# Experts' sums taken slot by slot, 64 columns of TensorE at a time, instead of two slots side by side

## The chip, the cores and the metric

One core of a Trainium2 chip runs the whole program. The metric is the device time of one execution in microseconds (us), with the median of several runs. Engines are TensorE (PE, with its weight loads PEld), VectorE (DVE), ScalarE (ACT), GpSimd (POOL) and SyncE (SP). They run their own instruction lists in order and are tied together by semaphores alone. DMA queues carry the transfers.

## What is computed

Two layers of a backbone over 256 latent tokens and 256 context tokens, 1024 channels. Each layer has a mixer (an input projection, a pooling mixer, latent attention, a bidirectional mLSTM, an output projection) and then an expert layer. The expert layer is what the first edit touches:

```python
def peer_ffn(h, w_q, subkeys, u_tab, v_tab):          # per block of 128 tokens
    q = (hb @ w_q).reshape(P, 8, 2, 128)
    s = einsum('phcd,hcnd->phcn', q, subkeys)         # 128 keys, two halves, 8 heads
    ...                                               # top 16 of 16 x 16 pairs -> 16 experts a head
    expert = i1 * 128 + i2
    a = gelu(einsum('pd,phkd->phk', hb, u_tab[expert]))
    w = softmax(best) * a
    return einsum('phk,phkd->pd', w, v_tab[expert])   # 8 x 16 = 128 experts a token
```

The second edit touches one RMS norm over the 384 channels of the low-rank query, `rms_norm(zq, q_a_norm)`, a mean of squares over three blocks of 128 channels.

## The kernel before

**Slots.** Tokens are held in tiles of 128. A tile has 128 slots: in each, 128 rows of 8 KB (u and v side by side, 1 MB in all) are gathered by an indirect DMA into one buffer (L546, `gather`). A slot serves 64 tokens with two heads' experts, so two neighbouring slots (an even and an odd one) serve the two halves of the tile. For every slot `dot` (L1269, VectorE) multiplies the u half with the tokens' rows and sums; `gated` (L844, L845, L848, ScalarE) makes the gate, the coefficient and `diag`, a 128x64 matrix that carries the coefficients; `values` (L1668, TensorE) multiplies `diag` with the v half and adds into `acc`, the even slot into its partitions 0 to 63 and the odd one into 64 to 127. A 1024-column row takes two matmuls of 512 columns; a float32 matmul is two records in the profile, each with a weight load. After the 128 slots of a tile ScalarE copies `acc` out (`sums_out`) and starts the next tile.

**Two loops.** `experts(0)` (layer 0) has four tiles, 512 slots, and a ring of six buffers (`fast`). `experts(1)` (layer 1) has two tiles, 256 slots, and twelve buffers (`fast` and six cut from `mix`). `v_used` counts slots whose sums are done; `free_pair(m)` is the count that frees slot m's buffer. It is awaited by the gather that reuses a buffer (L545), by ScalarE before it writes one of the eight `diag` again (L847), and by six weight loads of SyncE behind the last slots (L511).

**Work behind the slots.** In the first loop the rest of the program runs behind the slots: the mixer of the latent tokens of layer 0, the adaLN product of layer 1 (24 weight tiles), and the context's keys and values of layer 1. Each engine has these parts written as generators that yield the slot after which a step may be issued, and `behind.run(m)` issues all that is due. Positions: projections at slots 12 to 59 (three steps to a group of eight matmuls, L1404), memory stage of four heads 63 to 92, row products 98 to 122, attention 127 to 165, output projection 167 to 190, adaLN 206 to 253, a shorter mixer's norm and projections 272 to 313. The expert layer's query products (L1627) lie between slots too, a whole product at a time split in pieces, 0 to 47, 203 to 303, in the second loop 0 to 47. From slot 314 on there is nothing but the slots. TensorE's order in a slot is: key scores, query piece, tile turns, `behind.run(m)`, then at an odd m `values(e, m - 1)` for both slots of the pair.

**The norm.** `low_rank` on ScalarE squares the three blocks of `zqT` (two buffers `sq`: the third square waits until TensorE has used the first), on TensorE `sum_square` (L1376) adds them, on VectorE `mean` and `inverse` turn the sum into a factor, with ScalarE's `root` between. `at` is slot 42 for this norm in the mixer behind the slots.

Of the kernel before, what the change touches and what calls it, by code (L numbers as in the profile page):

```python
# [15 lines left out]
D = 1024  # L16
# [24 lines left out]
SLOTS = PH * PTOP  # L41
HALF = P // 2
# [15 lines left out]
DIAGS = 8  # L58
# [15 lines left out]
def groups(p):  # L74
    return GROUPS if PHASES[p][2] else KV_GROUPS


def group_of(p, name, n):
    return [g[:2] for g in groups(p)].index((name, n)) + 1
# [23 lines left out]
def in_at(g):  # L103
    return IN_AT + IN_STEP * g
# [160 lines left out]
def build(nc, x_in, c_in, par_in, con_in, w_in, wq_in, uq_in, pw_in, uv_tabs, out):  # L265
    with ExitStack() as ctx:
        def sb(name, shape, dt=F32):
            return ctx.enter_context(nc.sbuf_tensor(name, shape, dt))
# [4 lines left out]
        def signal(name, *counts):  # L273
            return Signal(ctx, nc, name, counts)

        bank = [ctx.enter_context(nc.psum_tensor(f"bank{i}", [P, 512], F32)) for i in range(6)]
        acc = ctx.enter_context(nc.psum_tensor("bank67", [P, 1024], F32))
# [27 lines left out]
        diag = sb("diag", [P, DIAGS, HALF])  # L305
# [71 lines left out]
        def slot(e, m):  # L377
            return rings[e][m % len(rings[e])]
# [15 lines left out]
            return 4 if PHASES[p][1] == 0 else 2  # L394

        def free_pair(m):
            return 2 * (m // 2) + 2


        c_loaded, con_loaded, loaded = sem("c_loaded"), sem("con_loaded"), sem("loaded")  # L400
# [51 lines left out]
        def each(n):  # L452
            return [n * nt for nt in nts]
# [5 lines left out]
        dotted, diag_ready, v_used = (signal(n, *each(SLOTS)) for n in ("dotted", "diag_ready", "v_used"))  # L459
# [96 lines left out]
        def _(a):  # L556
# [7 lines left out]
            def square(p, n, src):  # L564
                if n >= 2:
                    a.wait_ge(sq_used.sem, sq_used.at(p, n - 1))
                a.activation(sq[:, n % 2, :], src, ACT.Square).then_inc(sq_ready.sem, 1)

            def root(p, n):
                a.wait_ge(ms_ready.sem, ms_ready.at(p, n))  # L570
                a.activation(rms[:, :], rms[:, :], ACT.Sqrt).then_inc(rt_ready.sem, 1)
# [90 lines left out]
            def low_rank(p):  # L662
                at = in_at(group_of(p, "zkv", 1) - 1) + 3
                yield at + 1
                a.wait_ge(in_evac.sem, in_evac.at(p, group_of(p, "zkv", 1)))
                for k in range(2):
                    square(p, KC + k, zkvT[:, k, :])
                yield at + 5
                root(p, 2)
                if PHASES[p][2]:  # L670
                    at = in_at(group_of(p, "zq", 2) - 1) + 3
                    yield at + 1
                    a.wait_ge(in_evac.sem, in_evac.at(p, group_of(p, "zq", 2)))
                    for k in range(3):
                        square(p, KC + 2 + k, zqT[:, k, :])
                    yield at + 5
                    root(p, 3)

            def pooled(p):
# [230 lines left out]
        def _(v):  # L910
# [36 lines left out]
            def mean(p, n, squares_used, width):  # L947
                v.wait_ge(sq_used.sem, sq_used.at(p, squares_used))
                if n == 1 and p:
                    v.wait_ge(hx_ready.sem, hx_ready.starts[p])  # L950
                if n == 2:
                    v.wait_ge(hx_ready.sem, hx_ready.at(p, KC))
                if n == 3:
                    v.wait_ge(zn_ready.sem, zn_ready.at(p, 2))
                if n == 4:
                    v.wait_ge(zn_ready.sem, zn_ready.at(p, 5))
                v.tensor_scalar(rms[:, :], bank[3][:, 0:SEQ], 1.0 / width, EPS, ALU.mult, ALU.add).then_inc(ms_ready.sem, 1)

            def inverse(p, n):
                v.wait_ge(rt_ready.sem, rt_ready.at(p, n))  # L960
                link(v.reciprocal(rms[:, :], rms[:, :]))
# [48 lines left out]
            def low_rank(p):  # L1010
                l, s, whole = PHASES[p]

                def scaled(z, n, gains):
                    for k in range(n):
                        v.scalar_tensor_tensor(out=z[:, k, :], in0=z[:, k, :], scalar=par[:, l, gains + k:gains + k + 1],
                                               in1=rms[:, :], op0=ALU.mult, op1=ALU.mult).then_inc(zn_ready.sem, 1)

                at = in_at(group_of(p, "zkv", 1) - 1) + 3
                yield at + 4
                mean(p, 2, KC + 2, KVRANK)  # L1020
                yield at + 6
                inverse(p, 2)
                scaled(zkvT, 2, PB_KVN)
                if whole:
                    at = in_at(group_of(p, "zq", 2) - 1) + 3
                    yield at + 4
                    mean(p, 3, KC + 5, QRANK)
                    yield at + 6
                    inverse(p, 3)
                    scaled(zqT, 3, PB_QN)  # L1030

# [283 lines left out]
        def _(t_):  # L1315
# [58 lines left out]
            def sum_square(p, n, first, last):  # L1374
                t_.wait_ge(sq_ready.sem, sq_ready.at(p, n + 1))
                t_.matmul(bank[3][:, 0:SEQ], ones, sq[:, n % 2, :], start=first, stop=last).then_inc(sq_used.sem, 1)  # L1376
# [50 lines left out]
            def low_rank(p):  # L1427
                yield in_at(group_of(p, "zkv", 1) - 1) + 6
                t_.wait_ge(ms_ready.sem, ms_ready.at(p, 1))
                for k in range(2):  # L1430
                    sum_square(p, KC + k, k == 0, k == 1)
                if PHASES[p][2]:
                    yield in_at(group_of(p, "zq", 2) - 1) + 6
                    t_.wait_ge(ms_ready.sem, ms_ready.at(p, 2))
                    for k in range(3):
                        sum_square(p, KC + 2 + k, k == 0, k == 2)

            def pooling(p):
# [214 lines left out]
            def sums_turn(e, i, f):  # L1653
                t_.wait_ge(y_ready.sem, y_ready.at(e, i + 1))
                take_aside(x_part, x_part.at(e, 2 * i + f + 1))
                for j in range(4):
                    mm = t_.transpose(b_aside[:, j * P:(j + 1) * P], yrow[:, (4 * f + j) * P:(4 * f + j + 1) * P], ident)
                mm.then_inc(yt_mm.sem, 1)

            def values(e, m):  # L1660

                if m % SLOTS == 0 and m:
                    t_.wait_ge(y_ready.sem, y_ready.at(e, m // SLOTS))
                t_.wait_ge(diag_ready.sem, diag_ready.at(e, m + 2))
                for f in range(2):
                    for half in range(2):
                        n = m + half
                        mm = t_.matmul(acc[half * HALF:(half + 1) * HALF, f * 512:(f + 1) * 512], diag[:, n % DIAGS, :],  # L1668
                                       slot(e, n)[:, D + f * 512:D + (f + 1) * 512],
                                       start=(n % SLOTS < 2), stop=(n % SLOTS >= SLOTS - 2))  # L1670
                mm.then_inc(v_used.sem, 2)

            def experts(e, behind):
                nt = nts[e]
                answer = {slot_: u for u, slot_ in ASKED[e].items()}
                part_of = {slot_: (u, k0, k1) for slot_, u, k0, k1 in QUERIES[e]}
                query(e, 0, 0, KC)
                query(e, 1, 0, KC)
                for u in range(8):
                    key_scores(e, u)  # L1680
                    if u == 3:
                        for half in range(2):
                            for f in range(2):
                                rows_turn(e, 0, half, f)
                    if u + 2 < 8:
                        query(e, u + 2, 0, KC)
                for m in range(SLOTS * nt):
                    i, n = divmod(m, SLOTS)
                    if m - 2 in answer:
                        key_scores(e, answer[m - 2])  # L1690
                    if m in part_of:
                        query(e, *part_of[m])
                    if i and n == 0:
                        rows_turn(e, i, 1, 1)
                    if i and n in (4, 8):
                        sums_turn(e, i - 1, (n - 4) // 4)
                    if i + 1 < nt:
                        if n == 114:
                            rows_turn(e, i + 1, 0, 0)
                        if n == 117:  # L1700
                            rows_turn(e, i + 1, 0, 1)
                        if n == 124:
                            rows_turn(e, i + 1, 1, 0)
                    behind.run(m)
                    if m % 2:
                        values(e, m - 1)
                for f in range(2):
                    sums_turn(e, nt - 1, f)

# [108 lines left out]
```

## Time and profile before

| | us |
|---|---|
| median of 3 runs | 2892.78 |
| lowest, highest | 2888.32, 2907.57 |
| profiled execution | 2890.09 |
| its span, first to last instruction | 2888.3 |

All rows below come from the one profiled execution, whose time is 1.8 us above its span. Times in them are us from the start of the span. A row of the busy table has for each engine its busy time and the number of records; then PEclk, the clock granted to TensorE as a share of 2.4 GHz (it has two levels, 1.2 and 2.4, so 0.75 is half of the time at either), the mean busy share of the DMA engines, and the rate. Busy is the time in which at least one record of the engine ran, so matmuls that overlap count once. The first loop's dots run from 323 to 1884 and the second's from 2218 to 2872.

### The profile page before, as it was taken

The page shows a single profiled execution, that of the slowest core. Times are in us where ns is not written, and L with a number is a line of the kernel's source. Part 1 is how long each engine was busy: PE and PEld are TensorE (multiplying, and loading weights), DVE is VectorE, ACT ScalarE, POOL GpSimd, SP SyncE. Part 2 cuts the span into 40 slices and gives each one's busy share as a digit, 9 for nine tenths or more (in the row PEclk, how much of TensorE's full clock was granted, in tenths as well). Part 3 has the DMA queues.
Part 4 walks back from the last instruction along what each step waited for, and adds up shares of the span by engine and source line. Part 5 has one row for each costly group of instructions (what it writes and reads, how often), then busy time and mean ns, then how long its engine had stood idle before and what let it go on. Part 6 is the DMA issues. An engine that isn't in the chain of part 4 may idle for free.

```text
span 2888.3 us, 26625 instructions
## 1 busy us (share of the span) xinstructions
PE 2007.8 (70%) x8372; PEld 981.8 (34%) x8372; DVE 1638.7 (57%) x4029; ACT 1123.0 (39%) x3259; POOL 868.1 (30%) x772
## 2 busy tenths in 40 slices
PE   7988598767777777786555555587796865565555
PEld 4756455332343343342111111155574421111111
DVE  2252477668875644676666665432532777776664
ACT  3242263556663433354333333332331443343332
POOL 0000133334354322334344434300001444444442
PEclk9879899878899898898777777786698997787777
DMA  7520499989999999999999999931004999999997
GB/s 311 222 117 17 150 393 412 378 311 372 386 382 411 403 420 421 386 403 394 384 387 369 387 392 391 379 127 46 15 1 154 412 426 426 426 426 426 426 426 303
DMA packets 133660, 940.05 MB, mean 325 GB/s; under 512 B 14864, under 2 KB 16144, under 8 KB 23312
## 3 DMA queue, kind: packets, MB, share of 16 engines
q0 software_dynamic: 110592, 805.36, 69.1%
q1 hardware_dynamic: 22496, 130.31, 11.4%
q10 hardware_dynamic: 432, 2.70, 0.2%
q8 instruction: 66, 1.08, 0.1%
q14 instruction: 74, 0.61, 0.1%
HBM read 937.26 MB, written 1.05 MB: 325 GB/s over the span
## 4 chain that ended last, share of the span: by engine, by line
DMA 42%; PE 32%; DVE 9%; ACT 8%; issue 4%; POOL 4%; POOLq 0%; SPq 0%; DVEq 0%; ACTq 0%
DMA fast<-uv_dram,idx 38%; PE bank L1668 11%; DVE fast L1269 4%; PE bank L1627 4%; PE bank L1404 4%; DMA qring<-wq_dram 3%; POOL fast L546 3%; PE bank L1590 2%; PE bank L1482 2%; ACT diag L848 1%; PE bank L1398 1%; ACT coef L845 1%; PE bank L1637 1%; PE bank L1574 1%; PE bank L1376 1%
## 5 line engine op out<-in xcount | busy, mean ns | idle before, releaser
L546 POOL DMA_INDIRECT fast<-uv_dram,idx x642 | 726.2, 1131 | 1819.4 <-PE bank L1668 1051.9
L1668 PE MATMUL bank<-fast,diag 128*64 128x512 f32 x2568 | 826.7, 777 | 585.7 <-ACT diag L848 585.4
L1269 DVE SCALAR_TENSOR_TENSOR fast<-fast,hrow 128x1024 f32<-128x1024 f32 x642 | 785.8, 1224 | 597.5 <-DMA fast<-uv_dram,idx 590.2
L844 ACT ACTIVATE gact<-araw 128x1 f32<-128x1 f32 x768 | 155.0, 202 | 1089.7 <-DVE fast L1269 922.7
L1668 PEld LDWEIGHTS bank<-fast,diag 128*64 128x64 f32 x2568 | 188.3, 164 | 1110.3 <-ACT diag L848 834.0
L1627 PE MATMUL bank<-hT,qring 128*128 128x256 f32 x768 | 238.7, 443 | 76.6 <-DMA qring<-wq_dram 67.3
L848 ACT ACTIVATE diag<-con,coef 128x64 f32<-128x64 f32 x768 | 267.0, 348 | 25.1
L1668 PE MATMUL bank<-mix,diag 128*64 128x512 f32 x504 | 171.8, 818 | 113.3 <-ACT diag L848 113.3
L845 ACT ACTIVATE coef<-gact,wts 128x1 f32<-128x1 f32 x768 | 226.2, 295 | 24.9
L1627 PEld LDWEIGHTS bank<-hT,qring 128*128 128x128 f32 x768 | 152.2, 215 | 188.0 <-issue 93.6
L1269 DVE SCALAR_TENSOR_TENSOR mix<-mix,hrow 128x1024 f32<-128x1024 f32 x126 | 154.5, 1226 | 98.1 <-DMA mix<-uv_dram,idx 95.2
L546 POOL DMA_INDIRECT mix<-uv_dram,idx x126 | 141.7, 1125 | 161.7 <-PE bank L1668 137.2
L1668 PEld LDWEIGHTS bank<-mix,diag 128*64 128x64 f32 x504 | 38.2, 168 | 235.8 <-ACT diag L848 178.1
L1404 PE MATMUL bank<-hT,back 128*128 128x256 f32 (+1 forms) x336 | 84.0, 389 | 4.1 <-ACT hT L594 4.1
L1404 PE MATMUL bank<-hT,fast 128*128 128x256 f32 (+1 forms) x320 | 76.1, 394 | 4.8 <-ACT hT L594 4.8
L1065 DVE TENSOR_TENSOR mix<-con,bank 128x256 f32<-128x256 f32 x48 | 17.0, 415 | 103.7 <-PE bank L1482 64.0
L1482 PE MATMUL bank<-mix 128*128 128x65 f32 x272 | 54.2, 376 | 30.6 <-DVE mix L1075 30.6
L814 ACT ACTIVATE pq<-bank 128x256 f32<-128x256 f32 x48 | 18.2, 379 | 142.2 <-PE bank L1627 142.1
L1404 PEld LDWEIGHTS bank<-hT,back 128*128 128x128 f32 (+1 forms) x336 | 63.3, 190 | 17.9 <-issue 7.4
L844 ACT ACT_TABLE_LOAD x52 | 66.7, 1283 | 0.9
L1404 PEld LDWEIGHTS bank<-hT,fast 128*128 128x128 f32 (+1 forms) x320 | 61.1, 194 | 16.6 <-issue 7.3
L1482 PEld LDWEIGHTS bank<-mix 128*128 128x128 f32 x272 | 50.9, 286 | 42.3 <-issue 42.3
(222 smaller groups left out, 2337.4 us busy)
## 6 DMA issues: line engine op xcount, KB each, us to landing
fast<-w_dram SPq DMA_DIRECT2D x48, 1024.0 KB, 7.2
back<-w_dram SPq DMA_DIRECT2D x44, 1024.0 KB, 9.9
qring<-wq_dram SPq DMA_DIRECT2D x48, 576.0 KB, 8.2
fast<-uv_dram,idx POOLq DMA_INDIRECT x642, 9.9
fast<-uq_dram SPq DMA_DIRECT2D x4, 576.0 KB, 4.4
xT<-x_dram ACTq DMA_DIRECT2D x1, 2048.0 KB, 8.7
mix<-uv_dram,idx POOLq DMA_INDIRECT x126, 22.2
back<-uq_dram SPq DMA_DIRECT2D x2, 576.0 KB, 8.2
```

The lines of the kernel that those rows point to most:

```text
L546: g.indirect_dma_start(slot(e, m), None, uv_tabs[e], bass.IndirectOffsetOnAxis(idx[:, Q % 2, n:n + 1], 0)).then_inc(landed[m % R], 16)
L844: link(a.activation(gact[:, n:n + 1], araw[:, Q % 2, n:n + 1], ACT.Gelu))
L845: link(a.activation(coef[:, n:n + 1], gact[:, n:n + 1], ACT.Copy, scale=wts[:, Q % 2, n:n + 1]))
L848: a.activation(diag[:, m % DIAGS, :], two, ACT.Copy, scale=coef[:, n:n + 1]).then_inc(diag_ready.sem, 1)
L1269: v.scalar_tensor_tensor(out=u, in0=u, scalar=1.0, in1=hrow[:, (2 * i + half) % 3, :], op0=ALU.mult, op1=ALU.mult, accum_out=araw[:, Q % 2 ...
L1376: t_.matmul(bank[3][:, 0:SEQ], ones, sq[:, n % 2, :], start=first, stop=last).then_inc(sq_used.sem, 1)
L1398: mm = t_.matmul(bank[g % 2][:, 0:WT], hT[:, k, tile_cols(p, n)], w[:, k, :], start=(k == 0), stop=(k == KC - 1))
L1404: mm = t_.matmul(bank[g % 2][0:rows, 0:SEQ], w[:, k, o:o + rows], hT[:, k, cols(p)], start=(k == 0), stop=(k == KC - 1))
L1482: mm = t_.matmul(bank[3][:, o:o + MD + 1], mE[:, e, kc, q * P:(q + 1) * P], v1[:, kc % 2, h, :], start=(kc == kcs[0]), stop=(kc == kcs[-1]))
L1590: mm = t_.matmul(bank[b % 2][:, 0:SEQ], w[:, k, b % 2 * P:b % 2 * P + P], hT[:, k, cols(p)], start=(k == 0), stop=(k == KC - 1))
L1627: mm = t_.matmul(dst[:, 0:SEQ], qring[:, n % 2, k, :], hT[:, k, cols(p)], start=(k == 0), stop=(k == KC - 1))
L1668: mm = t_.matmul(acc[half * HALF:(half + 1) * HALF, f * 512:(f + 1) * 512], diag[:, n % DIAGS, :], slot(e, n)[:, D + f * 512:D + (f + 1) * ...
```

## The change

`values` takes one slot instead of two and is called after every slot. It waits for that slot's diagonal only, makes two matmuls of 512 columns into the slot's half of `acc`, and raises `v_used` by one. `free_pair(m)` becomes m + 1: a buffer is free when its own slot is summed. In the norm over the query's channels, the third square and all that follows it come two positions later on ScalarE, VectorE and TensorE (the square from `at + 1` to `at + 3`, where `at` counts slots; TensorE's third sum from 45 to 47).

```diff
         def free_pair(m):
-            return 2 * (m // 2) + 2
+            return m + 1
@@ scalar, low_rank
                     for k in range(3):
+                        if k == 2:
+                            yield at + 3
                         square(p, KC + 2 + k, zqT[:, k, :])
-                    yield at + 5
+                    yield at + 7
                     root(p, 3)
@@ vector, low_rank
-                    yield at + 4
+                    yield at + 6
                     mean(p, 3, KC + 5, QRANK)
-                    yield at + 6
+                    yield at + 8
                     inverse(p, 3)
@@ tensor, low_rank
                     for k in range(3):
+                        if k == 2:
+                            yield in_at(group_of(p, "zq", 2) - 1) + 8
                         sum_square(p, KC + 2 + k, k == 0, k == 2)
@@ tensor, values(e, m)
-                t_.wait_ge(diag_ready.sem, diag_ready.at(e, m + 2))
+                t_.wait_ge(diag_ready.sem, diag_ready.at(e, m + 1))
+                half = slice(m % 2 * HALF, m % 2 * HALF + HALF)
                 for f in range(2):
-                    for half in range(2):
-                        n = m + half
-                        mm = t_.matmul(acc[half * HALF:(half + 1) * HALF, f * 512:(f + 1) * 512], diag[:, n % DIAGS, :],
-                                       slot(e, n)[:, D + f * 512:D + (f + 1) * 512],
-                                       start=(n % SLOTS < 2), stop=(n % SLOTS >= SLOTS - 2))
-                mm.then_inc(v_used.sem, 2)
+                    mm = t_.matmul(acc[half, f * 512:(f + 1) * 512], diag[:, m % DIAGS, :], slot(e, m)[:, D + f * 512:D + (f + 1) * 512],
+                                   start=(m % SLOTS < 2), stop=(m % SLOTS >= SLOTS - 2))
+                mm.then_inc(v_used.sem, 1)
@@ tensor, experts
                     behind.run(m)
-                    if m % 2:
-                        values(e, m - 1)
+                    values(e, m)
```

## Rows read from the trace of the kernel before

**Rows 1.** Busy table by stage: us busy (records), PEclk, DMA share, GB/s

```profile
323.00:383.00 60.00, 41.01 (x173) 25.50 (x171) 28.39 (x79) 25.20 (x69) 17.93 (x15) 0.87 0.72 273
383.00:532.00 149.00, 134.61 (x602) 80.41 (x602) 100.43 (x239) 74.01 (x211) 52.89 (x49) 1.00 1.00 408
532.00:744.00 212.00, 147.80 (x559) 62.96 (x560) 150.84 (x368) 116.58 (x301) 76.28 (x67) 0.79 0.91 352
744.00:968.00 224.00, 169.00 (x759) 84.99 (x757) 171.10 (x451) 123.40 (x329) 98.11 (x81) 0.93 0.99 389
968.00:1247.00 279.00, 210.34 (x1177) 98.45 (x1176) 141.44 (x350) 101.86 (x323) 77.78 (x77) 0.89 1.00 410
1247.00:1345.00 98.00, 83.06 (x331) 42.73 (x329) 65.44 (x161) 51.52 (x146) 38.68 (x34) 0.93 1.00 400
1345.00:1884.00 539.00, 290.62 (x872) 69.82 (x872) 328.22 (x769) 188.88 (x620) 214.76 (x193) 0.75 0.98 385
2218.00:2357.00 139.00, 104.14 (x420) 51.41 (x418) 85.59 (x226) 53.06 (x179) 64.27 (x56) 0.89 0.99 407
2357.00:2872.00 515.00, 301.56 (x912) 71.87 (x912) 344.04 (x808) 195.89 (x648) 224.85 (x200) 0.76 1.00 420
```

**Rows 2.** The same stretches, L1269's records on VectorE alone, two a slot

```profile
323.00:383.00 60.00, 14.48 (x24) 0.87 0.72 273
383.00:532.00 149.00, 59.21 (x96) 1.00 1.00 408
532.00:744.00 212.00, 82.63 (x135) 0.79 0.91 352
744.00:968.00 224.00, 97.09 (x159) 0.93 0.99 389
968.00:1247.00 279.00, 95.82 (x157) 0.89 1.00 410
1247.00:1345.00 98.00, 39.47 (x66) 0.93 1.00 400
1345.00:1884.00 539.00, 240.64 (x390) 0.75 0.98 385
2218.00:2357.00 139.00, 58.72 (x96) 0.89 0.99 407
2357.00:2872.00 515.00, 255.53 (x415) 0.76 1.00 420
```

**Rows 3.** Chain of waits, 1618 to 1635: start us, us, what

```profile
1618.22 3.54 PE bank L1668 x8
...
1622.02 0.96 POOL fast L546
...
1623.28 9.08 DMA fast<-uv_dram,idx
...
1634.23 0.36 ACT diag L848
...
1634.63 3.29 PE bank L1668 x8
```

**Rows 4.** TensorE's timeline, crowded stage and lone one: start us, us, line

```profile
420.69 1.94 PE L1668 MATMUL bank<-fast,diag 128*64 128x512 f32 x8
422.56 0.70 PE L1627 MATMUL bank<-hT,qring 128*128 128x256 f32 x2
423.10 1.46 PE L1404 MATMUL bank<-hT,back 128*128 128x256 f32 x6
...
1628.68 3.41 PE L1668 MATMUL bank<-fast,diag 128*64 128x512 f32 x8 [3.57 <-ACT diag L848]
```

**Rows 5.** TensorE's timeline, first mixer: four records into one half; the first alone

```profile
211.59 0.65 PE L1574 MATMUL bank<-mix 128*64 128x128 f32 x4
...
211.59 0.32 PE L1574 MATMUL bank<-mix 128*64 128x128 f32 x1
```

**Rows 6.** Chain of waits in the memory stage, one link

```profile
580.22 5.40 PE bank L1668 x16
```

## The prediction

> **What bounds the kernel now.** I read the busy table by stage first [rows 1], cut where the expert loop changes its company, then the slots in each cut [rows 2], then the chain of waits and TensorE's timeline inside a stage [rows 3 to 5] and one link of the memory stage's chain [rows 6]. In rows 1 look at three columns together: PE busy against the length of the stretch, PEclk, and GB/s. Three kinds of stage appear.
>
> First, the second loop (layer 1), from 2357 to 2872: 420 GB/s with the DMA share at 1.00 [rows 1] and 415 of rows 2 over two (a dot and its read of the accumulator each make one record), so 207.5 slots in 515 us, 2.48 us a slot. The gathers set it; its twelve buffers keep the queues full. Nothing that TensorE does there matters as long as it needs under 2.48 us a slot.
>
> Second, the end of the first loop, 1345 to 1884: hardly any other work, 195 slots in 539 us, 2.76 us each, at 385 GB/s. The gathers are not at their rate here, 0.28 us a slot short of it. The chain [rows 3] says why: from one pair's sums at 1618.22 to the odd slot of a pair at 1634.63 are 16.4 us, the round trip of six buffers (6 x 2.74). It reads: the pair's sums 3.54 us, the gather of the even slot 0.96 us with its gap to 1623.28, the gather of the odd one 9.08 us to its landing, the dot, ScalarE's three steps ending with the diagonal, sums again. Both buffers of a pair come free at one moment, so the two gathers go out together and the second lands behind the first.
>
> Third, the stages in which TensorE carries a mixer and the queries behind the slots. From 383 to 532 it is busy 134.61 of 149 us at clock 1.00, and from 1247 to 1345 83.06 of 98 [rows 1]. There it is nearly the bound already, beside 408 and 400 GB/s.
>
> **The change, step by step.** *What a slot's sums cost.* Before, the eight records of a pair take 1.94 us at 2.4 GHz (420.69) and 3.41 us at 1.2 GHz (1628.68) [rows 4]. Are these eight one behind another? Four records of 128 columns into one half of the array, one behind the other, take 0.65 us, of which the first alone is 0.32 [rows 5]: each further one adds 0.11 us. Estimate from that: 512 columns add four times as much, 0.43 us; eight in a row would be some 3.6 us at 2.4 GHz, four some 1.9. The pair took 1.94, so its two halves of the array run side by side, in four steps. After the change a slot's four records all go to one half: four steps again, 1.94 us by itself. So a slot costs TensorE what a pair did. In a full queue the next line starts 1.87 us after the pair (420.69 to 422.56) [rows 4]; I charge 1.87 us more per pair of slots. The number of matmuls and weight loads is unchanged; only what overlaps changes.
>
> One rule bears on it. By rows 4 and 5 two column halves overlap when the instructions alternate. The Trainium skill (TensorEngine Tiling (Array Packing), Key Properties) says that tiles run independently, and that a change of tiling mode drains the engine. By its first half, which the pair in rows 4 bears out, slot m+1 could still run beside slot m where nothing stands between them; by its second, not where a full-width matmul stands between. The first half by itself is the third rival below; with it the per-pair charge is 0 instead of 1.87.
>
> *What it adds per stage.* Rows 1, PE busy, plus 1.87 us for each pair (records of rows 2 over four), against the length:
> - 383 to 532: 134.6 + 24 x 1.87 = 179.5 us in 149: +30. Between two pairs the queue holds a query piece (L1627) and projection matmuls (L1404) for each slot [rows 4], so no two slots' sums are neighbours and none of this overlaps.
> - 532 to 744: 147.8 + 33.75 x 1.87 = 210.9 in 212: just fits in sum. But part of it is a chain through TensorE in the memory stage: 16 records of sums, 5.40 us, stand in one link before the products of the next head [rows 6]. If no slots overlap there, that link costs up to 3.7 us more (two pairs) for each of the four heads, 15 us; if they do, nothing. I take 8.
> - 744 to 968: 169.0 + 39.75 x 1.87 = 243.3 in 224: +19.
> - 968 to 1247: 210.3 + 39.25 x 1.87 = 283.7 in 279: +5; from here the weights' DMA bounds most of it at 410 GB/s.
> - 1247 to 1345: 83.1 + 16.5 x 1.87 = 113.9 in 98: +16.
> - 323 to 383, 41.0 + 6 x 1.87 = 52.2 in 60: hidden, 0 to +5. I take 0.
> - the second loop's start, 2218 to 2357: 104.1 + 24 x 1.87 = 149.0 in 139: +10. The ring of twelve absorbs none of it, since it starts full and the gathers that follow go out only as slots are used up.
>
> Sum of the losses: 30 + 8 + 19 + 5 + 16 + 10 = 88 us. The busy times hold stretches at 1.2 GHz (PEclk 0.79 to 0.93 in four of these rows), which a busier engine would partly run at 2.4. With a clock of 1.00 the PE sums of 744 to 968 and of 1247 to 1345 shrink by a few per cent (169.0 x 0.07 is 12 us at the most, 83.1 x 0.07 is 6), and the one of 968 to 1247 vanishes. I take 15 us off for it: 73.
>
> *What it gives.* In 1345 to 1884 a buffer comes free with its own slot. The even slot's gather goes out a slot earlier, and the odd one no longer waits behind it (1622.02 to 1623.28, 1.26 us) nor lands behind it. The round trip of rows 3 loses those 1.26 us and up to a transfer (2.48 us): 16.4 - 3.7 = 12.7 us for six slots, 2.1 a slot, below the gathers' 2.48. So the gathers bind, as in the second loop: I take 2.50 us. 195 x (2.76 - 2.50) = 51 us. TensorE needs 1.94 us of each 2.50 at 2.4 GHz. The granted clock was 0.75 here with 290.62 of 539 us busy and 1.00 in 383 to 532 with 134.61 of 149 [rows 1]; I expect it in between, mostly at 2.4 GHz. In the crowded stages the earlier release gives nothing: there the sums themselves come late. From 2357 on nothing either.
>
> *The waits.* TensorE now waits for every diagonal where it waited for every second. Behind that wait stand the next slot's query piece, key scores and mixer matmuls, and for these ScalarE's copies and VectorE's masks. A diagonal comes with its slot, so the wait is no longer than one slot; its cost shows in the memory stage and is in the 8 us. The sums at a tile's first slot now wait for ScalarE's copy of the accumulator one slot sooner, four times in all: under 2.5 us each, covered by the six buffers.
>
> *The norm's third square* is not worth a term: the same instructions; the reader of the scaled tile (the q products) comes at slot 98, some fifty slots later, and in the phases that run alone only the order of short steps changes. 0, bounds -2 and +3. Without the move ScalarE, at an odd place, would wait for a sum of squares that stands behind a slot whose diagonal it has not made. No DMA is moved by it. SyncE's six loads behind the last slots are freed by single slots: 0.
>
> Sum against the profiled execution's own 2890.1: + 73 - 51 = +22 to +37 (with or without the clock's 15). I take +33, near the upper end, because sums of busy time leave out every gap that a dependence makes in a nearly full engine: 2923; the median of the runs shown is 2.7 above the profiled execution, so 2926.
>
> **Rivals.**
> 1. *The same mechanisms near balance.* If stages with spare time in their neighbours take up part of the 73, or the clock gives 15 more, the losses are 45 to 65 and the gain 51: 2880 to 2915. For it: DMA share 0.91 and clock 0.79 in 532 to 744. Against it: busy 90% at 383 to 532, with no slack behind.
> 2. *Slower by more: the clock.* If the granted clock stays near its present 0.75 in the lightly loaded stages, half the time at each level, and slots do not overlap, a slot takes (1.94 + 3.41)/2 = 2.7 us there, which is above 2.48. Then 1345 to 1884 gains nothing (+51 against the forecast) and 2357 to 2872 becomes TensorE's: 207.5 x (2.7 - 2.48) = +46. 2926 + 97 = 3023. It decides from a mean of 2.48 us a slot. For it: PEclk 0.75 and 0.76 in these two stretches now [rows 1]. Against it: 1.00 and 0.93 in the two that kept TensorE busiest.
> 3. *Faster: slots still run side by side.* If the array takes slot m+1's first half beside slot m's second, also around the mixer's matmuls, the losses go and only the gain is left: 2893 - 51 = 2842, with a little more from 383 to 1345 where six buffers bind too, 2835. It decides if the third kind of stage costs under 22 us. Against it: the full-width matmuls between the sums in rows 4.
> 4. *The change does nothing*: gathers already out early enough. Against it: 0.28 us a slot between the two loops at the same work. It is within rival 1.
>
> **Numbers.** Forecast (crowded stages lose more than the lone one gains, +15 to +70) 0.5; rival 1 0.2; rival 2 0.1; rival 3 0.2. A measurement of this kernel can tell about 1%, 29 us, from no change. Slower by over 1% (above 2922): 0.4 from the forecast and 0.1 from rival 2, 0.5. Faster by over 1% (below 2864): rival 3 and a tail, 0.22. Same: 0.28. Range 2842 to 3000: it leaves out most of rival 2 and half of rival 3. The forecast's own range is 2905 to 2965.
>
> **What would show it.** After: 383 to 532 grows to about 179 us with PE over 95% busy; the 33 slots before 1345 grow by a sixth; the lone stage goes at 2.50 us a slot and over 415 GB/s with PEclk above 0.85 and PE busy near 1.94 / 2.50 of the time; POOL's waits for TensorE there shrink; the second loop stays at 2.48 but starts 10 us later. A sums group of a slot alone at 2.4 GHz reads x4, 1.94 us. It would be wrong if two slots' records were seen to overlap between full-width matmuls (rival 3), if PEclk stayed at 0.75 with PE near 100% busy (rival 2), or if VectorE's or ScalarE's waits in the mixer grew more than TensorE's own work.

## The result, and the profile after

The changed kernel takes 2915.58 us (median of 8 runs, 2913.22 to 2922.37) against 2896.27 us for the one before in the same comparison: ratio 1.0069, 95% interval 1.0052 to 1.0087. It is slower by 19 us, 0.7%, which is under the 1% that the prediction called a change. The profiled execution has a span of 2917.0 us against 2888.3, 28.7 us more; the stages below are read from these two executions. Ratios and intervals are estimated from all runs of a comparison, and differ by up to 0.2% from the quotients of the medians. Below, the lone stage is slots 316 to 511 of the first loop, which have nothing behind them; in the crowded stages other work runs behind the slots.

The whole-program rows hide what happened; the engine's busy share rose from 70% to 83%, and the clock granted to it rose too. Page of the changed kernel, busy us by engine, then the granted clock in 40 slices in tenths:

```profile
PE 2420.5 (83%) x8372; PEld 1092.8 (37%) x8372; DVE 1634.2 (56%) x4029; ACT 1117.0 (38%) x3259; POOL 803.2 (28%) x772
...
PEclk9869799989999999999999999987698999999999
```

The busy table of the changed kernel, cut at the same slots as [rows 1] (the first loop's slot 12, 60, 127, 206, 284, 316 and 511, then the second loop's start and rest; columns as there):

```profile
400.00:573.00 173.00, 173.00 (x590) 86.97 (x589) 98.97 (x239) 73.11 (x210) 54.48 (x47) 1.00 0.92 346
573.00:778.00 205.00, 168.81 (x572) 68.99 (x571) 149.99 (x368) 116.38 (x301) 82.94 (x69) 0.93 0.92 362
778.00:1016.00 238.00, 214.19 (x743) 95.03 (x742) 171.07 (x451) 122.21 (x329) 79.83 (x78) 0.99 0.95 367
1016.00:1300.00 284.00, 261.48 (x1184) 110.88 (x1182) 141.27 (x348) 97.56 (x314) 82.82 (x77) 0.97 0.99 403
1300.00:1412.00 112.00, 106.41 (x332) 47.79 (x331) 65.93 (x162) 54.29 (x155) 34.27 (x32) 0.98 0.95 359
1412.00:1909.00 497.00, 382.54 (x883) 98.52 (x881) 326.99 (x768) 188.98 (x620) 187.85 (x193) 1.00 1.01 418
2245.00:2389.00 144.00, 125.76 (x385) 52.56 (x383) 84.86 (x227) 46.51 (x159) 58.53 (x51) 0.94 0.98 392
2389.00:2902.00 513.00, 403.38 (x948) 106.03 (x946) 342.98 (x806) 199.45 (x666) 202.58 (x204) 1.00 1.00 422
```

Against [rows 1]: the first stage of projections went from 149 to 173 us, and TensorE is busy in all 173 of them, while the DMA rate fell from 408 to 346 GB/s. The lone stage went the other way, from 539 to 497 us and from 385 to 418 GB/s, and its granted clock from 0.75 to 1.00. The rest of the second loop stayed at its gathers' pace.

TensorE's timeline of the changed kernel, in the crowded stage and in the lone one (start us, us, line, shape, records):

```profile
464.09 1.93 PE L1671 MATMUL bank<-fast,diag 128*64 128x512 f32 x4
465.95 0.70 PE L1631 MATMUL bank<-hT,qring 128*128 128x256 f32 x2
466.49 1.46 PE L1406 MATMUL bank<-hT,back 128*128 128x256 f32 x6
467.88 1.93 PE L1671 MATMUL bank<-fast,diag 128*64 128x512 f32 x4
...
1621.27 1.93 PE L1671 MATMUL bank<-fast,diag 128*64 128x512 f32 x4 [0.55 <-ACT diag L850]
1623.75 1.93 PE L1671 MATMUL bank<-fast,diag 128*64 128x512 f32 x4 [0.55 <-ACT diag L850]
```

Four records of one slot take 1.93 us, and eight of a pair took 1.94 in [rows 4]. In the crowded stage a slot's work adds up to 3.79 us (464.09 to 467.88) with nothing idle. In the lone stage one group follows the other every 2.48 us.

But where nothing stands between two slots' sums, they still run side by side. The same timeline in the memory stage, two slots behind one another, at the lower clock for most of the time:

```profile
637.12 3.27 PE L1671 MATMUL bank<-fast,diag 128*64 128x512 f32 x8
```

Eight records in 3.27 us: not more than a pair written as a pair took in [rows 4], 3.41 us. The memory stage's chain of waits in the changed kernel, one head (start us, us, what), and below it the line of the kernel before that stands one head after [rows 6]:

```profile
623.60 5.34 PE bank L1671 x12
...
630.65 1.86 PE bank L1671 x4
...
637.19 3.25 PE bank L1671 x8
...
647.53 5.34 PE bank L1671 x12
```

```profile
604.32 3.59 PE bank L1668 x8
```

Three slots take 5.34 us here and two 3.25, so they overlap; one stands alone between other matmuls (630.65). A head takes 23.9 us (623.60 to 647.53) against 24.1 before (580.22 to 604.32).

In the first slots another loss shows. The chain of waits of the changed kernel there:

```profile
366.69 1.93 PE bank L1671 x4
368.62 1.06 PE bank L1631 x4
369.68 0.45 PE bank L1378 x2
...
370.15 0.42 ACT mix L567
...
371.45 0.36 ACT diag L850
...
371.85 1.93 PE bank L1671 x4
```

This is a closed round through two engines: TensorE's sums, a query piece and a sum of squares, then ScalarE's squares (L567), which wait for that sum and stand before the next diagonal, then sums again. In these slots TensorE waits for every diagonal and is idle for 1.31 us of each 5.16 (its timeline has `[1.31 <-ACT diag L850]` at 371.85). From the sums of slot 1 to those of slot 5 the changed kernel takes 20.1 us (361.53 to 381.67), the one before 15.1 from the pair of slots 0 and 1 to that of 4 and 5 (352.14 to 367.21).

The time of each stage in every kernel that ran, from the start of one slot's dot to that of another, in us of its one profiled execution:

| kernel | 0-12 | 12-60 | 60-127 | 127-206 | 206-284 | 284-316 | 316-511 | second loop, first 48 | rest |
|---|---|---|---|---|---|---|---|---|---|
| before | 60.3 | 149.2 | 211.5 | 224.1 | 279.2 | 98.6 | 538.5 | 139.7 | 514.4 |
| changed | 70.9 | 173.2 | 205.0 | 238.2 | 284.6 | 111.4 | 497.6 | 144.2 | 514.1 |
| norm_alone | 60.8 | 148.1 | 214.0 | 220.8 | 282.1 | 101.3 | 542.2 | 140.4 | 514.4 |
| crowd_single | 68.0 | 173.2 | 203.0 | 239.8 | 284.8 | 109.8 | 534.5 | 139.4 | 514.2 |
| lone_single | 58.8 | 150.2 | 211.8 | 221.6 | 281.6 | 100.0 | 495.6 | 139.6 | 514.4 |
| lone_late | 60.5 | 150.7 | 217.8 | 225.1 | 280.1 | 102.8 | 498.6 | 138.9 | 514.4 |
| warm_pair | 58.3 | 149.8 | 212.7 | 224.5 | 283.8 | 98.9 | 500.4 | 141.0 | 513.9 |
| pair_in_row | 62.1 | 147.0 | 209.3 | 222.9 | 281.5 | 100.7 | 536.9 | 139.7 | 513.8 |
| mixed | 60.7 | 150.2 | 203.2 | 222.3 | 280.2 | 97.7 | 496.1 | 138.9 | 514.2 |
| second_single | 60.2 | 148.9 | 205.7 | 223.7 | 282.5 | 98.0 | 534.8 | 145.4 | 514.2 |
| split | 58.9 | 149.1 | 203.8 | 218.0 | 278.8 | 96.7 | 495.1 | 141.6 | 514.4 |
| split_late | 61.0 | 146.7 | 204.3 | 219.5 | 277.9 | 97.0 | 496.4 | 139.7 | 514.3 |

How far single executions of the same code differ can be read where kernels are alike: 97.7 to 102.8 in 284 to 316 and 205.7 to 217.8 in 60 to 127 among those with pairs there. The 6.5 us between before and changed in 60 to 127 are, by themselves, no more than that spread. But all five kernels that sum each slot for itself there have 203.0 to 205.0, below every one of the seven with pairs. So this stage too seems to gain some 8 us in the mean.

### The profile page after: what moved, and what is told of

Its sections match the earlier page's. It is cut to its first block, busy times and chain, and to the rows that moved or that the text cites. A ratio compares the mean times of both kernels' runs of the same rounds, so it can differ in the third digit from the quotient of the medians.

```text
span 2917.0 us, 26625 instructions
## 1 busy us (share of the span) xinstructions
PE 2420.5 (83%) x8372; PEld 1092.8 (37%) x8372; DVE 1634.2 (56%) x4029; ACT 1117.0 (38%) x3259; POOL 803.2 (28%) x772
## 4 chain that ended last, share of the span: by engine, by line
PE 48%; DMA 33%; ACT 9%; DVE 7%; issue 2%; POOL 0%; SPq 0%; DVEq 0%; POOLq 0%; ACTq 0%
DMA fast<-uv_dram,idx 26%; PE bank L1671 19%; PE bank L1631 7%; PE bank L1406 5%; DMA mix<-uv_dram,idx 4%; PE bank L1594 3%; DVE fast L1271 3%; DMA qring<-wq_dram 2%; PE bank L1486 2%; PE bank L1400 2%; PE bank L1641 1%; ACT diag L850 1%; ACT L846 1%; ACT coef L847 1%; PE bank L1378 1%
## 5 line engine op out<-in xcount | busy, mean ns | idle before, releaser
L1671 PE MATMUL bank<-fast,diag 128*64 128x512 f32 x2568 | 1211.9, 618 | 270.0 <-ACT diag L850 265.4
L546 POOL DMA_INDIRECT fast<-uv_dram,idx x642 | 675.9, 1053 | 1901.3 <-PE bank L1671 1186.8
L1671 PEld LDWEIGHTS bank<-fast,diag 128*64 128x64 f32 x2568 | 300.2, 138 | 1002.7 <-ACT diag L850 571.4
L1671 PE MATMUL bank<-mix,diag 128*64 128x512 f32 x504 | 237.3, 604 | 52.7 <-ACT diag L850 51.0
L850 ACT ACTIVATE diag<-con,coef 128x64 f32<-128x64 f32 x768 | 267.1, 348 | 25.1
L1631 PEld LDWEIGHTS bank<-hT,qring 128*128 128x128 f32 x768 | 145.0, 210 | 235.4 <-issue 154.0
L546 POOL DMA_INDIRECT mix<-uv_dram,idx x126 | 127.2, 1009 | 174.0 <-PE bank L1671 165.0
L1671 PEld LDWEIGHTS bank<-mix,diag 128*64 128x64 f32 x504 | 58.5, 136 | 215.0 <-ACT diag L850 133.4
L1406 PEld LDWEIGHTS bank<-hT,fast 128*128 128x128 f32 (+1 forms) x320 | 60.5, 192 | 16.2 <-issue 7.3
L959 DVE TENSOR_SCALAR rms<-bank 128x256 f32<-128x256 f32 x14 | 5.9, 424 | 105.2 <-PE bank L1378 105.2
```

The source lines that it names most:

```text
L546: g.indirect_dma_start(slot(e, m), None, uv_tabs[e], bass.IndirectOffsetOnAxis(idx[:, Q % 2, n:n + 1], 0)).then_inc(landed[m % R], 16)
L850: a.activation(diag[:, m % DIAGS, :], two, ACT.Copy, scale=coef[:, n:n + 1]).then_inc(diag_ready.sem, 1)
L1406: mm = t_.matmul(bank[g % 2][0:rows, 0:SEQ], w[:, k, o:o + rows], hT[:, k, cols(p)], start=(k == 0), stop=(k == KC - 1))
L1631: mm = t_.matmul(dst[:, 0:SEQ], qring[:, n % 2, k, :], hT[:, k, cols(p)], start=(k == 0), stop=(k == KC - 1))
L1671: mm = t_.matmul(acc[half, f * 512:(f + 1) * 512], diag[:, m % DIAGS, :], slot(e, m)[:, D + f * 512:D + (f + 1) * 512], start=(m % SLOTS < ...
```

## The experiments

**1. The norm's edit alone.** The kernel before with the norm's lines of the diff and nothing else.

> The kernel before with the norm's edit alone: sums still in pairs, the third square and all behind it two positions later on the three engines. In the two profiles the first loop's first dot came 5.8 us later after the change and the stretch between the loops was 1.2 us longer, and both hold a run of this norm outside the slots. If the edit costs that, this kernel is 5 to 7 us slower than before (ratio about 1.002). If the edit is free, as the prediction had it, the ratio is 1.000 within 0.1% and the 5.8 us are a difference between two executions.

Measured: 2901.07 us against 2896.31, ratio 1.0005, interval 0.9986 to 1.0024. The edit has no measurable price. The interval by itself would leave room for 5.8 us (0.24% is 7 us). The first dot does not point to the edit either: it starts at 327.0 to 329.5 us in the three kernels with the edit, 322.7 in the one before, and anywhere from 322.0 to 329.8 in the eight others without it. The 5.8 us are within what single executions differ by.

**2. Slot by slot in the lone stage only.**

```diff
+        def alone(e, m):
+            return e == 0 and m >= 316
...
-                    if m % 2:
+                    if alone(e, m):
+                        value(e, m)
+                    elif m % 2:
                         values(e, m - 1)
```

`value` is the new body of `values`, and a buffer is free at m + 1 where `alone` holds.

> Sums slot by slot only in the first loop from slot 316 on, where nothing runs behind the slots; pairs everywhere else, norm as before. By the forecast's mechanism (a slot alone costs TensorE what a pair did, which hurts only where TensorE is full) this keeps the gain of the lone stage, 41 us in the two profiles, and has none of the losses: about 2855 us, ratio 0.986. Rival: the gain there comes from buffers and queues left in another state by the crowded stages before it; then it would be under 20 us, above 2875.

Measured: 2848.73 us, ratio 0.9833 (0.9802 to 0.9865). The lone stage by itself is worth 43 us in the profile (538.5 to 495.6) and 48 in the medians. It doesn't need the crowded stages before it to be changed.

**3. The complement: slot by slot only below slot 316.** `alone` is `e == 0 and m < 316`, with the norm's edit.

> The complement: slot by slot only for slots 0 to 315 of the first loop, with the norm's edit; pairs from 316 on and in the second loop. Forecast's mechanism: only losses, the stages' differences in the two profiles summed (10.6 + 24 - 6.6 + 14.1 + 5.3 + 12.8 = 60 us): about 2956 us, ratio 1.021. If successive slots' sums mostly overlapped in the array, or the losses were an echo of something in the second loop, it would be under 2925.

Measured: 2951.1 us, ratio 1.0197 (1.0163 to 1.0232), 55 us slower. The lone stage of this kernel, with pairs, beside that of experiment 2 (busy table, columns as above; first this kernel, then the other):

```profile
1408.00:1943.00 535.00, 300.47 (x880) 70.84 (x879) 328.26 (x770) 189.30 (x621) 216.78 (x193) 0.75 0.98 387
```

```profile
1351.00:1846.00 495.00, 381.00 (x876) 98.07 (x876) 326.77 (x768) 188.28 (x616) 189.02 (x192) 0.99 1.01 420
```

Losses and gain are separate: 55 us lost below slot 316, 48 gained above, 7 in sum; the changed kernel has 19. The second loop's start (experiment 8) may be some 5 of the other 12. The rest can't be told from nothing: the three ratios are known to 5 us (changed kernel), 9 and 10 us.

**4. The gain without the early release.** As experiment 2, but the gather waits for both slots of the old pair.

```diff
-                    g.wait_ge(v_used.sem, v_used.at(e, free_pair(e, m - R)))
+                    g.wait_ge(v_used.sem, v_used.at(e, 2 * ((m - R) // 2) + 2))
```

> As lone_single, slot by slot from slot 316 on, but the gather that reuses a buffer waits until both slots of the old pair are summed, as before. If the gain of the lone stage comes from the buffers coming free one by one, it goes away: 2.75 us a slot or more there and about 2893 us in all. If it comes from TensorE's clock, which rose from 0.75 to 1.00 in this stage and takes the last sums before a release from 3.4 to 1.9 us, most of it stays: about 2.60 us a slot, 2865 us or less.

Measured: 2863.54 us, ratio 0.9876 (0.9841 to 0.9910). In the stage itself 498.6 us, 2.56 us a slot, against 495.6 with the early release and 538.5 before. So 40 of the 43 us stay although no buffer is given back before its pair is summed. The prediction's account, that the earlier release makes the gain, falls here. (The medians of experiments 2 and 4 are 15 us apart. In the two profiles only 3 of 17 us lie in the lone stage, the others where the code is the same, 60 to 127 above all; the intervals of the two ratios overlap.) The chain of waits of this kernel in the stage (start us, us, what):

```profile
1632.74 1.95 PE bank L1682 x4
...
1634.95 0.93 POOL fast L549
...
1636.18 9.22 DMA fast<-uv_dram,idx
...
1647.26 0.36 ACT diag L851
...
1647.65 1.95 PE bank L1682 x4
```

This is the chain of [rows 3], link by link, with two gathers that go out together (1634.95, 1636.18) and the second landing 9.22 us later. Only TensorE's link is shorter, 1.95 us instead of 3.54. The round trip is 14.91 us instead of 16.41, which over six slots is 2.485 us, the gathers' own pace.

**5. The gain with pairs and a busier TensorE.** The kernel before, with unused work added from slot 336 on.

```diff
+                    if e == 0 and m >= 336 and m % 2 == 0:
+                        for _ in range(2):
+                            t_.matmul(bank[0][:, :], ident, con[:, 0:512], start=True, stop=True)
                     if m % 2:
                         values(e, m - 1)
```

> The kernel before, pairs everywhere, but from slot 336 of the first loop TensorE makes two unused full-width matmuls of 512 columns from constants before each pair's place (about 1.8 us at 2.4 GHz, into a bank nobody reads then). It keeps the engine about as busy as slot-by-slot sums do, without freeing any buffer earlier. If the clock makes the lone stage's gain, the clock goes to about 1.00 there, a pair takes 1.94 us instead of 3.4, and the pace falls from 2.76 to some 2.60 us a slot: 2866 us. If the earlier release makes it, the pace stays above 2.70 and the time above 2882 us.

Measured: 2855.68 us, ratio 0.9877 (0.9860 to 0.9893). Work that nobody reads makes the kernel 36 us faster. Busy table of the lone stage and TensorE's timeline in it:

```profile
1358.00:1858.00 500.00, 378.28 (x1224) 115.97 (x1224) 327.12 (x768) 188.14 (x616) 214.71 (x192) 0.96 1.01 413
```

```profile
1561.53 1.94 PE L1668 MATMUL bank<-fast,diag 128*64 128x512 f32 x8 [0.47 <-ACT diag L848]
1563.40 1.98 PE L1707 MATMUL bank<-con 128*128 128x512 f32 x4
1566.49 1.94 PE L1668 MATMUL bank<-fast,diag 128*64 128x512 f32 x8 [1.12 <-ACT diag L848]
1568.36 1.98 PE L1707 MATMUL bank<-con 128*128 128x512 f32 x4
```

The clock over the stage is 0.96 (the added work begins 20 slots into it) instead of 0.75, each pair takes 1.94 us, and the stage 500.4 us. Its round trip in the chain of waits is 14.91 us as well (1631.34 to 1646.25). From both sides, then: the release taken away leaves 40 of 43 us, the clock alone brings 38. In this stage slot-by-slot sums help because they keep TensorE at work for 381 of 495 us in place of 291 of 539, in shorter gaps (0.55 us instead of up to 3.57), and its clock stays at 2.4 GHz. The Trainium skill (TensorE: Matmul & The Clock Gate, Part 1) says that the throttled state is the default and activity lifts it; these runs agree.

**6. The pair's matmuls in another order.**

```diff
-                for f in range(2):
-                    for half in range(2):
+                for half in range(2):
+                    for f in range(2):
```

> The kernel before with the two loops inside a pair's sums exchanged: the even slot's two matmuls first, then the odd slot's two, back to back, released together. If TensorE starts the second slot's half beside the first's although the instructions no longer alternate, the eight records take 4 steps as before, 1.94 us, and the time is that of before. If it starts them in order and each waits for its own half, a part overlaps: 7 steps, about 3.2 us; if nothing overlaps, 8 steps, 3.6 us. In both of these the crowded stages lose nearly what the change loses, 40 to 60 us, without any gain in the lone stage: 2935 to 2960 us.

Measured: 2895.46 us against 2891.86, ratio 1.0006 (0.9986 to 1.0025). Timeline in the crowded stage:

```profile
427.54 1.94 PE L1668 MATMUL bank<-fast,diag 128*64 128x512 f32 x8
```

Eight records in 1.94 us with the even slot's four written first. The instructions need not alternate: the odd slot's half starts beside the even slot's. So the changed kernel does not lose by the order within the sums.

**7. Slot by slot in two stages.** `alone` is `e == 0 and (60 <= m < 126 or m >= 316)`.

> Slot by slot where TensorE has room (first loop, slots 60 to 125 and from 316 on), pairs elsewhere and in the second loop. The changed kernel was 6.6 us faster than the one before in slots 60 to 126 and 41 us in the lone stage. If both stages stand for themselves, 2893 - 41 - 7 = 2845 us, ratio 0.983, 7 us below the kernel that does it in the lone stage alone. If the 6.6 us were a difference between two executions or came from the crowded stage before, it is equal to that kernel, about 2853.

Measured: 2843.21 us, ratio 0.9849 (0.9828 to 0.9870). Against experiment 2 (0.9833, interval 0.9802 to 0.9865) there is no difference to be told. In its profile 60 to 127 takes 203.2 us, one of the five values below all those with pairs (table above); the time of the kernel alone doesn't decide whether that stage gains. What would make the gain was not isolated. It is not the release, since experiment 10 has 204.3 us there without it; the granted clock in these stretches is 0.89 to 0.94 where slots are summed alone, and 0.78 to 0.81 in the seven with pairs.

**8. Slot by slot in the second loop only.** `alone` is `e == 1`.

> Slot by slot in the second loop only. Forecast: its first 48 slots carry the queries, TensorE gets 45 us more to do in a stretch of which it is busy 104 of 139 us, and the time rises by 5 to 10 us (the two profiles: 4.5), ratio 1.002 to 1.003; the rest of the loop is bound by the gathers and stays. Rival: the twelve buffers hide that too, ratio 1.000.

Measured: 2897.9 us against 2893.19, ratio 1.0013 (0.9992 to 1.0034). The profile has 145.4 us for the first 48 slots, where the kernels with pairs there have 138.9 to 141.0. By the stage some 5 us; by the ratio not to be told from nothing.

**9. Back to back, but each slot for itself.** The kernel before, with two calls of `value` in the place of the pair, and a buffer free at m + 1.

```diff
                     if m % 2:
-                        values(e, m - 1)
+                        value(e, m - 1)
+                        value(e, m)
```

> One slot at a time with its own wait and its own release, as in the changed kernel, but both slots' sums are issued at the odd slot, one behind the other, after the work behind both slots (where the kernel before has its pair); norm as before. It differs from the changed kernel in the place of the even slot's sums alone. If the crowded stages' loss comes from full-width matmuls standing between two slots' sums, it goes away and the lone stage keeps its gain: 2893 - 48 = 2845 us, perhaps 5 to 8 less where the clock also rises between slots 60 and 127. If the loss comes from the second wait and the second release per pair, it stays: about 2905 us or more.

Measured: 2827.79 us against 2893.19, ratio 0.9763 (0.9731 to 0.9796). It has as many waits and releases as the changed kernel and differs from it in the place of the even slot's sums (and in the norm, which is worth nothing by experiment 1), and it is faster than the changed kernel by some 88 us in the medians (by the two ratios 1.0069 - 0.9763 = 3.1%) and than the one before by 65. That is 9 to 17 us below what was expected: besides the lone stage (43 us) its profile has 8 us less than before in 60 to 127 and 6 less in 127 to 206. Its timeline in the crowded stage and in the lone one:

```profile
431.37 1.94 PE L1679 MATMUL bank<-fast,diag 128*64 128x512 f32 x8
433.25 0.70 PE L1627 MATMUL bank<-hT,qring 128*128 128x256 f32 x2
433.78 1.46 PE L1404 MATMUL bank<-hT,back 128*128 128x256 f32 x6
435.08 0.59 PE L1627 MATMUL bank<-hT,qring 128*128 128x256 f32 x2
435.51 1.03 PE L1404 MATMUL bank<-hT,back 128*128 128x256 f32 x4
436.46 1.94 PE L1679 MATMUL bank<-fast,diag 128*64 128x512 f32 x8
...
1567.53 1.93 PE L1679 MATMUL bank<-fast,diag 128*64 128x512 f32 x4 [0.71 <-ACT diag L848]
1569.96 1.93 PE L1679 MATMUL bank<-fast,diag 128*64 128x512 f32 x4 [0.50 <-ACT diag L848]
```

Where TensorE is behind, both diagonals are ready and the two slots run side by side in 1.94 us, across the second slot's own wait and the first one's release. Where it is ahead, each slot goes as its diagonal comes. The same code does what each stage wants. Moving the even slot's sums takes away two things at once, the full-width matmuls between two slots' sums and the early wait for the even diagonal. In slots 12 to 60 only the first can count: the changed kernel's TensorE never waits there (173.00 of 173 us busy). In 0 to 12 the wait shows by itself (the round of 5.16 us above). Where TensorE still waits for diagonals, as in 127 to 206 (22 us in all), no run separates the two.

**10. The same with the late release.** Experiment 9 with the gather's wait of experiment 4.

> As split, but a gather waits until both slots of the old pair are summed, as in the kernel before. Runs so far: in the lone stage a late release cost 3 of 43 us and a pair beside filler work gained 38 of them, so there the clock explains nearly all. If that holds in the crowded stages too, this kernel is within 5 us of split (2828 us). If there the release one by one is what split gains (8 us between slots 60 and 127, 6 between 127 and 206), it is 12 to 20 us above split, about 2840 to 2848.

Measured: 2836.79 us, ratio 0.9809 (0.9786 to 0.9832). The medians are 9 us apart, but the two kernels ran in different comparisons: against its own kernel before, one gains 65 us and the other 60, and the intervals of the ratios overlap. The profiles' stages agree within 2.5 us each. So most of what this form gains, too, is not the release. The 9 us lie between the two cases expected, and whether the release is worth up to that much here stays open.

## Why the prediction came out as it did

The time lies in the range and the sign is right; 2915.6 is 10 us under the forecast's 2926. The likeliest case said slower by over 1%. The measured 0.7% lies low in the forecast's own range (2905 to 2965) and at the upper edge of rival 1 (2880 to 2915), which had losses and gain nearer to balance. By its steps:

**What a slot's sums cost: right.** 1.93 us for x4, as worked out from [rows 4, 5]. In slots 12 to 60 TensorE's busy time in the sums alone went from 46.53 us to 90.27, 43.7 more, where 24 x 1.87 = 44.9 was charged. All of its work took 173.0 us where 179.5 was expected.

**The losses: right in kind, too large in sum.** Experiment 3 measures them below slot 316 at 55 us in medians, where the list without the second loop's start has 78, and 63 after the clock's 15. Term by term from the table: 12 to 60, +30 expected, +24 measured; 127 to 206, +19 and +14; 206 to 284, +5 and +5; 284 to 316, +16 and +13; second loop's start, +10 and +5. The first twelve slots were the miss in the other direction: 0 was taken, since 52.2 us of work fitted into 60, and crowd_single shows +8 and the changed kernel +11. TensorE is not overfull there, it is busy for 52.4 of 71 us. What the prediction had wrong is the step on the waits: it named the wait for every diagonal but put its whole cost in the memory stage. It costs in the first slots, where the round through ScalarE's squares now closes once a slot: 5 us in the four slots read above. What makes the rest of these 8 to 11 us stays open.

**The memory stage: wrong.** +8 was taken for sums that would stand one behind the other in its chain. Adjacent slots overlap (637.12, experiments 6 and 9), and a head takes 23.9 us against 24.1 before, so there was nothing to pay. The table has no loss in 60 to 127 in any kernel, and more likely a gain. The rule of the Trainium skill that was weighed (TensorEngine Tiling (Array Packing), Key Properties), that tiles run independently, is borne out for adjacent groups, and rival 3's mechanism exists. What stands against it is a full-width matmul between the two, as the prediction said: experiment 9 puts the two slots' sums side by side again, and the crowded stages are back at the times of before, 12 to 60 above all, where no wait takes part.

**What it gives: near in size, wrong in cause, so the size is partly luck.** 51 us were expected in the lone stage; 41 came in the profile of the changed kernel, 48 in the medians of experiment 2. The size came from the gathers' pace as the floor, which holds whatever brings the stage down to it. But the step put it to the buffers' release: "The round trip of rows 3 loses those 1.26 us and up to a transfer". Experiment 4 takes that away and keeps 40 of 43 us; experiment 5 gives the clock alone and has 38. The sum that was not made is short: in [rows 3] the only link that the clock touches is the sums' 3.54 us, and with 1.95 in its place the round trip is 16.4 - 1.6 = 14.8 us, six times 2.47. That alone reaches the gathers' pace, after which an earlier release has little left to give (3 us by experiment 4). What the release would give at a clock of 0.75 no run shows. The rise of the clock was expected in the text, but only as a condition for TensorE to keep up, not as the gain.

**The rival of the clock: refuted.** The granted clock did not stay at 0.75 but went to 1.00, with half of the array in use at a time.

**The last choice.** +33 was taken near the top of +22 to +37. The terms as measured by the stages are 11 + 24 - 7 + 14 + 5 + 13 + 5 - 41 = +24, the medians say +19. The lower end would have been nearer. That the total fits so well is in part luck: losses set too high, a gain set too high and the first slots' loss left out offset one another.

## What to carry to other kernels

Where an engine's work runs in parts of an array, what stands between two such parts decides: keep them adjacent when the engine is behind, and give each its own wait so that it can start alone when the engine is ahead (experiment 9, 2.4% faster than before). Before a gain is put to a buffer's earlier release, take each link of the round trip and ask what the clock does to it; here TensorE, half idle at 0.75, made the round trip longer too, and a run with unused work in the gaps tells whether that is the cause. A stage's sum of busy time shows where an added load can't fit, but not that it does: a new wait can close a round through another engine while TensorE is idle.

## What was not expected of the hardware

Work that nobody reads made the kernel 36 us faster (1.2%): 1.98 us of matmuls in each gap of TensorE took its granted clock in the lone stage from 0.75 to 0.96. Two groups of matmuls into different halves of the array ran side by side even when written one whole group after the other, 1.94 us for eight records, and also with a wait and a release between them.
